# RWKV quarters: products of the joins, the values and the inverse's application laid over four array quadrants, with other work put between them

## The chip, the cores and the metric

The kernel runs on one core of one Trainium2 chip. The metric is the device time of one execution in microseconds (us). The PE (TensorE) makes the matrix products, ACT (ScalarE), DVE (VectorE) and POOL (GpSimd) the rest; SP issues the weight loads. The PE writes into eight PSUM banks of 128 partitions x 512 words. One fp32 product of the program shows as two PE records in the trace, a transpose or a product in the fp32r type as one.

## The reference

The program is three blocks for 512 tokens of width 1024. The change lies in the second block, in an RWKV-7 time mix: 16 heads of width 64, a state per head that is updated token by token.

```python
def step(state, inp):                      # state: heads x 64 x 64
    r_t, w_t, k_t, v_t, a_t, b_t = inp     # a = -kk, b = kk * a_gate
    sa = jnp.einsum('bhvk,bhk->bhv', state, a_t)
    state = (state * w_t[:, :, None, :] + sa[..., None] * b_t[:, :, None, :]
             + v_t[..., None] * k_t[:, :, None, :])
    return state, jnp.einsum('bhvk,bhk->bhv', state, r_t)
...
y = wkv7_scan(r_h, heads(decay), k_h, v_h, -kk, kk * a_h)
y = ((y - mean) * lax.rsqrt(var + GN_EPS)).reshape(B, S, RWKV_DIM)   # a norm per head
y = y * ln_w.astype(f32) + ln_b.astype(f32)
bonus = jnp.sum(r_h * k_h * r_k.astype(f32), axis=-1, keepdims=True) * v_h
y = y + bonus.reshape(B, S, RWKV_DIM)
return (y * g.astype(f32)).astype(z.dtype) # g = sigmoid(gd) @ g2, the gates
```

## The kernel before

The scan is done in chunks of 64 tokens. Within a chunk the tokens' effect on each other is a triangular system of 64 x 64; with its inverse known, the whole chunk is matrix products, and only a short chain of eight state steps runs from chunk to chunk.

The work goes in four quarters (`for q in range(4)` in each engine's program), each for four heads h = 0..3, or 2n + x with n, x in 0, 1. A tile of 128 tokens (c = 0..3) holds two chunks, z = 0 on partitions 0 to 63 and z = 1 on 64 to 127. Most tiles of this stage are `[128, c, h, 64]`: the rows of both chunks on the partitions, and for each tile and head 64 columns. Products of this stage therefore have 64 rows and 64 outputs: each uses one quadrant of the PE array, chosen by the half of the partitions it reads and the half it writes.

After the projections k, r and v of a quarter and the small products low and gram, PE makes the inverse `invt` of each chunk's system. Blocks of 16 come from powers (`pa`, `pd`, up to `pd` of level 3). Two joins then put blocks of 16 together to 32 and of 32 to 64: for each level, `mu` = `e_m` x `invt`, copied by ACT to `mid`; `my` = `inv` x `mid`, added by DVE into `invt`. `inv` is the transpose of `invt`, made by DVE (`turn_inverse`). All of these go in two halves g (tiles 2g and 2g + 1) of eight products of a chunk pair each, made by `pair_of_tiles`. Then:

- `x0` = `ka` x values, copied by ACT into the first 64 columns of `x_a`; `ta` turns `a_r` into the last 64;
- `w` = `invt` x `x_a`, 128 columns, one bank for each tile c, copied out by ACT (c = 0 to 2) and DVE (c = 3) to `w_a`;
- `e` and `s` from `w_a` (DVE adds them up), the gates products (`gates_part`), and `y`;
- `st`, the chain of state steps, between them pieces of the next quarter's k projection (`some_channels`) on PE.

`rwkv_out` turns the result of the quarter before. POOL makes `e_m` (semaphore `between_ready`), multiplies the normed result of the quarter before with its gates (`rwkv_o_ready`) and prepares the gates.

The order of the work is written by hand in every engine's program. Each result of PE is a job with a number; the list of `job` calls gives the order, a job's bank is its number modulo eight, `claim` waits for the reader of the bank's job before, `fill` signals the last product, `wait_full` and `read` stand at the reader, and `wait_read` waits for it. Every matmul of the program goes through line 857 and every transpose of this stage through line 870, every ACT operation through line 1548; so profiles are read by tiles and by time. Of DVE, 2173 is a sum or product of two tensors, 2612 the turning of the inverse, 2658 the copy of w's last bank. Line 694 issues small loads on ACT's queue. The placing of the products is this, before and in the y stage (`both` is the pair of partition halves):

```python
# pair_of_tiles: output half z, from half z
ins = mm(ps(j)[z, at_:at_ + DH], w[z, c, h, :], x[z, c, h, :])
# y: output half z xor x
for n, x, h, _ in heads:
    for z in range(2):
        mm(o[c, n, x][both[z ^ x]], kr[both[z], c, h, :], v_by_head[both[z], c, h, :], c == 0 and n == 0, False)
```

Weights come in pieces: SP loads them, ACT rounds a high part (`weights_hi`), DVE takes the low part (`weights_lo`), each some pieces ahead (`stream_to`).

Of the kernel before, what the change touches and what calls it, by code (L numbers as in the profile page):

```python
# [36 lines left out]
ALU = mybir.AluOpType  # L37
# [65 lines left out]
def build_program(nc, d, x_saved, fc_saved, out):  # L103

    with ExitStack() as ctx:
# [311 lines left out]
        for q in range(4):  # L417
# [23 lines left out]
            for g in range(2):  # L441
                job(q, "pd", g, 3)
            for g in range(2):
                job(q, "x0", g)
            for g in range(2):
                job(q, "mu", g, 0)
            twice(q, "ta")
            for g in range(2):
                job(q, "my", g, 0)
            for g in range(2):  # L450
                job(q, "mu", g, 1)
            for g in range(2):
                job(q, "my", g, 1)
            if q:
                twice(q - 1, "out")
            for c in range(TT):
                job(q, "w", c)
# [3 lines left out]
            job(q, "g", 0)  # L461
            twice(q, "s")
            job(q, "g", 1)
# [390 lines left out]
        def _(pe):  # L854
# [327 lines left out]

            def rwkv_out(q):

                pe.wait_ge(sem("rwkv_o_ready"), q + 1)
                for n in range(2):
                    transposes(J[q, "out", n], [y_q[:, c, n * P:(n + 1) * P] for c in range(TT)])

            def gates_part(q, g):

                j = J[q, "g", g]
                claim(pe, j)
                for c in range(2):
                    tok = slice((2 * g + c) * P, (2 * g + c + 1) * P)
                    mm(ps(j)[:, c * 256:(c + 1) * 256], lo_g1[:, tok], g2_a[:, 256 * q:256 * q + 256], True, False)
                    ins = mm(ps(j)[:, c * 256:(c + 1) * 256], lo_g2[:, tok], g2_b[:, 256 * q:256 * q + 256], False, True)
                fill(j, ins)
# [7 lines left out]
            for q in range(4):  # L1205
# [82 lines left out]
                pe.wait_ge(sem("v_centred"), q + 1)  # L1288
                for g in range(2):
                    for c in (2 * g, 2 * g + 1):  # L1290
                        for x in range(2):
                            wait_read(pe, J[q, "gram", c, x])
                    pair_of_tiles(J[q, "x0", g], g, ka, v_by_head)


                for g in range(2):
                    wait_read(pe, J[q, "pd", g, 3])
                    pe.wait_ge(sem("between_ready"), 4 * q + g + 1)
                    pair_of_tiles(J[q, "mu", g, 0], g, e_m[0], invt)
                for n in range(2):  # L1300
                    transposes(J[q, "ta", n], [a_r[:, n, c, 0, :] for c in range(TT)])
                for g in range(2):
                    pe.wait_ge(sem("inv_turned"), 4 * q + g + 1)
                    wait_read(pe, J[q, "mu", g, 0])
                    pair_of_tiles(J[q, "my", g, 0], g, inv, mid)
                for g in range(2):
                    wait_read(pe, J[q, "my", g, 0])
                    pe.wait_ge(sem("between_ready"), 4 * q + g + 3)
                    pair_of_tiles(J[q, "mu", g, 1], g, e_m[1], invt)
                for g in range(2):  # L1310
                    pe.wait_ge(sem("inv_turned"), 4 * q + g + 3)
                    wait_read(pe, J[q, "mu", g, 1])
                    pair_of_tiles(J[q, "my", g, 1], g, inv, mid)
# [3 lines left out]

                for n in range(2):
                    wait_read(pe, J[q, "ta", n])
                for c in range(TT):  # L1320
                    if c % 2 == 0:
                        wait_read(pe, J[q, "my", c // 2, 1])
                        wait_read(pe, J[q, "x0", c // 2])
                    j = J[q, "w", c]
                    claim(pe, j)
# [3 lines left out]
                    fill(j, ins)  # L1329
# [3 lines left out]
                for g in range(2):  # L1333
                    for z in range(2):
                        claim(pe, J[q, "e", g, z])
# [1651 lines left out]
```

## Time and profile before

| what | value |
|---|---|
| three runs | 1526.01, 1526.58 (median), 1530.64 us |
| the profiled execution, its own time | 1530.57 us |
| its span, first to last instruction | 1528.8 us |
| PE busy | 1494.9 us, 98% |
| DVE, ACT, POOL busy | 890.8, 694.6, 119.5 us |
| mean granted clock of PE | 0.992 of full |

A row of a timeline gives start, duration, engine, line, operation, output and input tiles and shape, and how many instructions are merged in it; in brackets the idle time of the engine before it and what ended that. The duration of a PE row runs to the modelled end of its last product and overhangs the start of the next row a little; the time that a burst costs is the distance of the starts. All SBUF tiles of this stage lie in one buffer, shown as `arena`, some in `extra`. `ACTq` is ACT's queue of issues. Times in the timelines are us from the start of the span. The four quarters' stages of small products end near 399, 494, 584 and 676 us.

### The profile page before, as it was taken

To read this page: it belongs to the slowest core of one execution; us is meant where nothing else is said; L and a number is where in the kernel's file an instruction comes from. 1 tells how busy PE (TensorE), PEld (TensorE's weight loads), DVE (VectorE), ACT (ScalarE), POOL (GpSimd) and SP (SyncE) were. 2 spreads that over 40 slices of the span, in tenths; PEclk is the share of its full clock that TensorE was granted. 3 is DMA by queue.
4 is the path that set the end of the run, shared out by engine and by line. 5 is a ranking of instruction groups with operands and counts; after the bars stand their busy time and mean duration, and the time that the engine had idled before them with its cause. 6 is when DMAs were issued, how large, how long until landed. Compare 5 with 4: busy or idle time off the path is not lost.

```text
span 1528.8 us, 31329 instructions
## 1 busy us (share of the span) xinstructions
PE 1494.9 (98%) x13362; PEld 1227.0 (80%) x13362; DVE 890.8 (58%) x1665; ACT 694.6 (45%) x1267; POOL 119.5 (8%) x78
## 2 busy tenths in 40 slices
PE   6999999999999999999999999999999999999998
PEld 5877867778789797888787778888887888888886
DVE  3658465547475574843347996442456777777223
ACT  5563265573352644434337997422244433334132
POOL 0004000002222142231000000000000000000000
PEclk9999999999999999999999999999999999999999
DMA  6232205331020111207221001232441323232331
GB/s 218 84 111 84 83 29 166 129 100 46 10 79 11 56 38 30 57 11 176 83 63 48 2 2 43 84 110 84 163 138 42 110 83 110 83 110 84 96 111 69
DMA packets 110970, 123.68 MB, mean 81 GB/s; under 512 B 22344, under 2 KB 94664, under 8 KB 110448
## 3 DMA queue, kind: packets, MB, share of 16 engines
q1 hardware_dynamic: 107904, 114.26, 23.8%
q10 hardware_dynamic: 2928, 7.41, 1.4%
q8 instruction: 107, 1.75, 0.5%
q14 instruction: 31, 0.25, 0.1%
HBM read 117.45 MB, written 4.21 MB: 80 GB/s over the span
## 4 chain that ended last, share of the span: by engine, by line
PE 87%; ACT 5%; DVE 4%; issue 2%; DMA 1%; SPq 0%; DVEq 0%; ACTq 0%
PE bank L857 83%; PE bank L870 4%; ACT arena L1548 3%; DVE arena L2173 1%; ACT L1548 1%; DMA arena<-in_x 1%; DVE weights_lo L2173 1%; DMA weights<-in_w_in 1%; ACT weights_hi L1548 1%; DVE arena L2539 0%; DVE arena L2176 0%; DVE arena L2347 0%; DVE arena L2263 0%; ACT extra L1548 0%; ACT h_hi L1548 0%
## 5 line engine op out<-in xcount | busy, mean ns | idle before, releaser
L1548 ACT ACTIVATE arena<-bank 128x512 f32<-128x512 f32 (+3 forms) x399 | 215.1, 568 | 492.0 <-PE bank L857 456.2
L857 PE MATMUL bank<-h_hi,weights_hi 128*128 128x512 f32 x1000 | 400.3, 400 | 4.6 <-DVE weights_lo L2173 2.9
L857 PE MATMUL bank<-h_lo,weights_hi 128*128 128x512 f32 x1000 | 391.4, 391 | 0.0
L857 PE MATMUL bank<-h_hi,weights_lo 128*128 128x512 f32 x1000 | 391.3, 391 | 0.0
L2173 DVE TENSOR_TENSOR weights_lo<-weights,weights_hi 128x1024 fp32r<-128x1024 f32 x179 | 220.4, 1234 | 268.2 <-ACT weights_hi L1548 259.1
L857 PE MATMUL bank<-arena 64*64 64x64 f32 (+6 forms) x6978 | 320.5, 249 | 6.0 <-ACT arena L1548 3.5
L857 PEld LDWEIGHTS bank<-arena 64*64 64x64 f32 (+3 forms) x6978 | 256.4, 140 | 65.0 <-issue 54.6
L1548 ACT ACTIVATE weights_hi<-weights 128x1024 fp32r<-128x1024 f32 x179 | 188.5, 1054 | 150.8 <-PE bank L857 149.2
L857 PEld LDWEIGHTS bank<-h_hi,weights_hi 128*128 128x128 f32 x1000 | 189.0, 189 | 52.3 <-issue 6.8
L857 PEld LDWEIGHTS bank<-h_hi,weights_lo 128*128 128x128 f32 x1000 | 188.8, 189 | 40.2
L857 PEld LDWEIGHTS bank<-h_lo,weights_hi 128*128 128x128 f32 x1000 | 189.1, 189 | 36.6
L1548 ACT ACTIVATE arena<-arena,stat 128x128 f32<-128x128 f32 (+4 forms) x172 | 101.3, 597 | 20.0 <-PE bank L857 10.1
L2173 DVE TENSOR_TENSOR arena<-bank,arena 128x512 f32<-128x512 f32 (+3 forms) x120 | 64.2, 568 | 59.1 <-ACT arena L1548 36.3
L870 PE MATMUL bank<-const,arena 128*128 128x128 f32 x552 | 72.3, 277 | 0.6 <-issue 0.6
L857 PE MATMUL bank<-weights_hi,act_hi 128*128 128x512 f32 x176 | 68.5, 389 | 0.0
L857 PE MATMUL bank<-weights_hi,act_lo 128*128 128x512 f32 x176 | 68.5, 389 | 0.0
L857 PE MATMUL bank<-weights_lo,act_hi 128*128 128x512 f32 x176 | 68.5, 389 | 0.0
L2176 DVE SCALAR_TENSOR_TENSOR ff_c<-arena,par,ff_c 128x512 f32<-128x512 f32 x88 | 66.2, 752 | 3.1
L870 PEld LDWEIGHTS bank<-const,arena 128*128 128x128 f32 x552 | 60.1, 141 | 9.6 <-issue 7.5
L2263 DVE CUSTOM_DVE_ANT_0 arena<-bank,arena 128x128 f32<-128x128 f32 (+3 forms) x144 | 61.9, 486 | 9.2 <-PE bank L857 7.0
L2180 DVE TENSOR_SCALAR arena<-arena,stat 128x512 f32<-128x512 f32 (+4 forms) x174 | 60.3, 407 | 1.8
L2181 DVE TENSOR_SCALAR ff_c<-arena,par 128x512 f32<-128x512 f32 x44 | 24.1, 547 | 60.0 <-ACT arena L1548 59.6
(191 smaller groups left out, 1654.9 us busy)
## 6 DMA issues: line engine op xcount, KB each, us to landing
weights<-in_w_in SPq DMA_DIRECT2D x38, 1024.0 KB, 5.4
weights<-in_ffn_up SPq DMA_DIRECT2D x22, 1024.0 KB, 5.1
weights<-in_ffn_down SPq DMA_DIRECT2D x10, 1024.0 KB, 5.1
weights<-in_w_out SPq DMA_DIRECT2D x4, 1024.0 KB, 5.1
arena<-in_w_out SPq DMA_DIRECT2D x4, 1024.0 KB, 9.3
weights<-in_w_in SPq DMA_DIRECT2D x16, 256.0 KB, 4.6
weights<-in_w_branch_rwkv SPq DMA_DIRECT2D x4, 1024.0 KB, 5.1
weights<-in_w_branch_nsa SPq DMA_DIRECT2D x4, 1024.0 KB, 5.1
```

The source lines that it names most:

```text
L857: return pe.matmul(o, w, x, start=first, stop=last)
L870: ins = pe.transpose(ps(j)[:, i * P:(i + 1) * P], t, ident)
L1548: return act.activation(o, i, f, **kw)
L2173: return dve.tensor_tensor(o, a, b, op)
L2176: return dve.scalar_tensor_tensor(o, a, s, b, op0, op1)
L2180: return dve.tensor_scalar(o, a, s1, None, op0)
L2181: return dve.tensor_scalar(o, a, s1, s2, op0, op1)
L2263: ins = dve.tensor_tensor_reduce(out=unit(probs, 4 * s + n)[:, 0:w], in0=ps(j)[:, at_:at_ + w], in1=table, scale=1.0, scalar=3.0e38, op0=A ...
```

## The change

The products of the joins, of `x0` and of `w` are laid out like those of y: heads with n = 0 write the half that they read, heads with n = 1 the other one. The two n have a bank each, and the four products (n, z) follow one another. What comes out crossed is put back where it is next read: `turn_inverse` turns the inverse of the heads with n = 1 into the other half (three transposes in place of one), so that `my` comes out straight; ACT's copy of x0 and DVE's copy of `w` for n = 1 cross back (two copies of 64 partitions in place of one of 128). Sums and copies of the joins become two of 256 columns for one of 512.

The order changes too. `x0` moves from ahead of mu0 to between the two halves of my0. The gates are cut into four parts, ahead of each half of my1, behind `w` and behind `e`. The first part of the next k projection moves from behind y to ahead of it. DVE makes the sums of pd3 for both halves before it turns either, and takes the two low pieces of the next k behind its `w` copies. ACT copies the first half of the gates ahead of the results of the quarter before, for which it first waits for `rwkv_o_ready`.

```diff
             for g in range(2):
-                job(q, "x0", g)
+                joins("mu", 0, g)
+            twice(q, "ta")
+            joins("my", 0, 0)
+            twice(q, "x0")
+            joins("my", 0, 1)
             for g in range(2):
-                job(q, "mu", g, 0)
...
+                joins("mu", 1, g)
+            job(q, "g", 0)
...
+                joins("my", 1, g)
             if q:
                 twice(q - 1, "out")
...
+            for g in range(2):
+                for n in range(2):
+                    job(q, "w", g, n)
+            job(q, "g", 1)
...
+            def join(q, kind, lev, g, w, x):
+
+                for n in range(2):
+                    claim(pe, J[q, kind, g, n, lev])
+                for c in range(2):
+                    for y in range(2):
+                        for n in range(2):
+                            j, h, at_ = J[q, kind, g, n, lev], 2 * n + y, (2 * c + y) * DH
+                            for z in range(2):
+                                ins = mm(ps(j)[both[z ^ n], at_:at_ + DH], w[both[z], 2 * g + c, h, :], x[both[z], 2 * g + c, h, :])
+                            if c == y == 1:
+                                fill(j, ins)
...
-            def gates_part(q, g):
-
+            def gates_of(q, i):
+
+                g, c = i // 2, i % 2
                 j = J[q, "g", g]
...
+                if c == 0:
+                    claim(pe, j)
+                tok = slice(i * P, (i + 1) * P)
...
-                pe.wait_ge(sem("v_centred"), q + 1)
-                for g in range(2):
...
-                    pair_of_tiles(J[q, "x0", g], g, ka, v_by_head)
...
-                    pair_of_tiles(J[q, "mu", g, 0], g, e_m[0], invt)
+                    join(q, "mu", 0, g, e_m[0], invt)
                 for n in range(2):
                     transposes(J[q, "ta", n], [a_r[:, n, c, 0, :] for c in range(TT)])
+                pe.wait_ge(sem("inv_turned"), 4 * q + 1)
+                joined(q, "mu", 0, 0)
+                join(q, "my", 0, 0, inv, mid)
+                pe.wait_ge(sem("v_centred"), q + 1)
...
+                            for z in range(2):
+                                ins = mm(ps(j)[both[z ^ n], at_:at_ + DH], ka[both[z], c, h, :], v_by_head[both[z], c, h, :])
...
+                pe.wait_ge(sem("inv_turned"), 4 * q + 2)
+                joined(q, "mu", 0, 1)
+                join(q, "my", 0, 1, inv, mid)
                 for g in range(2):
...
+                    joined(q, "my", 0, g)
+                    pe.wait_ge(sem("between_ready"), 4 * q + g + 3)
+                    join(q, "mu", 1, g, e_m[1], invt)
                 for g in range(2):
...
+                    gates_of(q, g)
                     pe.wait_ge(sem("inv_turned"), 4 * q + g + 3)
...
+                    joined(q, "mu", 1, g)
+                    join(q, "my", 1, g, inv, mid)
                 if q:
                     rwkv_out(q - 1)
...
-                    for h in range(4):
-                        for z in both:
-                            ins = mm(ps(j)[z, h * P:(h + 1) * P], invt[z, c, h, :], x_a[z, c, h, :])
...
+                    for c in (2 * g, 2 * g + 1):
+                        for x in range(2):
+                            for n in range(2):
+                                j, h, at_ = J[q, "w", g, n], 2 * n + x, (2 * (c % 2) + x) * P
+                                for z in range(2):
+                                    ins = mm(ps(j)[both[z ^ n], at_:at_ + P], invt[both[z], c, h, :], x_a[both[z], c, h, :])
...
+                gates_of(q, 2)
...
-                gates_part(q, 0)
+                gates_of(q, 3)
...
-                gates_part(q, 1)
...
                 claim(pe, j_next)
+                some_channels(j_next, w_next, (0,))
                 o = {}
...
                 claim(pe, st)
-                some_channels(j_next, w_next, (0,))
...
+            def keep_mid(q, lev, g):
+
+                for n in range(2):
+                    j = J[q, "mu", g, n, lev]
+                    wait_full(act, j)
+                    o = mid[:, 2 * g:2 * g + 2, 2 * n:2 * n + 2].rearrange("p c x v -> p c (x v)")
+                    read(j, run(o, ps(j)[:, 0:256].rearrange("p (c x) -> p c x", c=2), ACT.Copy))
...
+                for n in range(2):
+                    to_heads(J[q, "x0", n], x_a[:, :, 2 * n:2 * n + 2, 0:DH], n)
                 phase_loads(act, "ln", L_LN[q])
                 for g in range(2):
-                    to_pair(J[q, "mu", g, 1], g, mid)
+                    keep_mid(q, 1, g)
+                if q:
+                    act.wait_ge(sem("rwkv_o_ready"), q)
+                copy_out(J[q, "g", 0], g_q[:, 0:2, :].rearrange("p c x -> p (c x)"))
...
+                    dve.transpose(pairs(inv, slice(0, P), 0), pairs(invt, slice(0, P), 0))
+                    for z in range(2):
+                        ins = dve.transpose(pairs(inv, sides[1 - z], 2), pairs(invt, sides[z], 2))
+                    ins.then_inc(sem("inv_turned"), 1)
...
                     sum_into(J[q, "pd", g, 3], g, invt)
-                    turn_inverse(J[q, "pd", g, 3], g)
                 for g in range(2):
                     wait_read(dve, J[q, "pd", g, 3])
...
+                    turn_inverse(g)
...
+                    join_sum(1, g)
+                for g in range(2):
+                    j = J[q, "w", g, 1]
+                    wait_full(dve, j)
+                    for z in range(2):
+                        to, at_ = slice(DH * z, DH * z + DH), slice(DH - DH * z, P - DH * z)
+                        ins = dve.tensor_copy(w_a[to, 2 * g:2 * g + 2, 2:4].rearrange("p c x v -> p c (x v)"),
+                                              ps(j)[at_, :].rearrange("p (c x) -> p c x", c=2))
+                    read(j, ins)
                 stream_to(next_k)
```

## Rows read from the trace of the kernel before

**Rows 1.** The page, parts 1 and 4: PE's share, and the ending chain by engine.

```profile
PE 1494.9 (98%) x13362; PEld 1227.0 (80%) x13362; DVE 890.8 (58%) x1665; ACT 694.6 (45%) x1267; POOL 119.5 (8%) x78
...
PE 87%; ACT 5%; DVE 4%; issue 2%; DMA 1%; SPq 0%; DVEq 0%; ACTq 0%
```

**Rows 2.** Timeline of PE, quarter 3: x0, mu0, then my0 to my1, out, w.

```profile
649.75 2.03 PE L857 MATMUL bank<-extra,arena 64*64 64x64 f32 x64
651.62 2.03 PE L857 MATMUL bank<-arena 64*64 64x64 f32 x64
...
654.60 6.20 PE L857 MATMUL bank<-arena 64*64 64x64 f32 x192
660.74 1.09 PE L870 MATMUL bank<-const,extra 128*128 128x128 f32 x8
661.76 7.77 PE L857 MATMUL bank<-arena 64*64 64x128 f32 x208
```

**Rows 3.** Timeline of PE, quarter 3: gates, y, k projection, first state step.

```profile
671.22 1.99 PE L857 MATMUL bank<-arena 128*128 128x256 f32 x8
673.14 1.16 PE L857 MATMUL bank<-extra,arena 64*64 64x64 f32 x64
674.12 1.11 PE L857 MATMUL bank<-arena 64*64 64x64 f32 x64
675.16 0.50 PE L857 MATMUL bank<-h_hi,weights_hi 128*128 128x512 f32 x1
...
676.06 0.45 PE L857 MATMUL bank<-arena 64*64 64x64 f32 x8
```

**Rows 4.** Timeline of all engines, quarter 3: DVE, ACT and POOL at the joins.

```profile
649.10 0.69 DVE L2173 TENSOR_TENSOR arena<-arena,bank 128x512 f32<-128x512 f32 x1 [0.54 <-PE bank L857]
...
649.83 0.71 DVE L2612 STREAM_TRANSPOSE arena<-arena 128x512 f32<-128x512 f32 x1
...
651.83 0.60 ACT L1548 ACTIVATE arena<-bank 128x512 f32<-128x512 f32 x1 [0.34 <-PE bank L857]
...
653.28 2.36 POOL L2111 TENSOR_TENSOR extra<-extra,arena 128x1024 f32<-128x1024 f32 x1
...
654.72 0.34 ACTq L694 DMA_DIRECT2D arena<-in_g_ln_w  x1
...
655.09 0.45 ACTq L694 DMA_DIRECT2D arena<-in_g_ln_b  x1
655.87 0.69 DVE L2173 TENSOR_TENSOR arena<-arena,bank 128x512 f32<-128x512 f32 x1 [4.01 <-PE bank L857]
```

**Rows 5.** Timeline of all engines, quarter 3: low pieces, w copies, sums of e.

```profile
661.52 2.35 DVE L2173 TENSOR_TENSOR weights_lo<-weights,weights_hi 128x1024 fp32r<-128x1024 f32 x2
...
662.90 0.60 ACT L1548 ACTIVATE arena<-bank 128x512 f32<-128x512 f32 x1 [0.38 <-PE bank L857]
...
665.52 0.69 DVE L2658 COPY arena<-bank 128x512 f32<-128x512 f32 x1 [1.65 <-PE bank L857]
666.45 2.74 DVE L2173 TENSOR_TENSOR arena<-bank,arena 128x256 f32<-128x256 f32 x8 [0.24 <-PE bank L857]
```

**Rows 6.** Timeline of PE, quarter 3: a gram set alone, and gram mixed with pairs.

```profile
630.87 0.90 PE L857 MATMUL bank<-arena 64*64 64x64 f32 x32
631.70 0.50 PE L857 MATMUL bank<-h_hi,weights_hi 128*128 128x512 f32 x1
...
633.29 4.11 PE L857 MATMUL bank<-arena 64*64 64x64 f32 x160
```

**Rows 7.** Groups by shape, whole span: a DVE sum of half the width.

```profile
L2173 DVE TENSOR_TENSOR arena<-bank,arena 128x256 f32<-128x256 f32 x32 | 11.0, 416 | 0.9 <-PE bank L857 0.9
```

**Rows 8.** Timeline of ACT, 684 to 700: copies of 64 partitions, 256 columns.

```profile
690.54 1.53 ACT L1548 ACTIVATE arena<-bank 64x256 f32<-64x256 f32 x4
```

**Rows 9.** Window of PE, quarter 1: length, busy, granted clock, DMA share, GB/s.

```profile
466.00:468.00 2.00, 2.00 (x46) 0.51 0.00 0
```

**Rows 10.** Timeline of PE, quarter 1: x0 at that time.

```profile
467.76 2.80 PE L857 MATMUL bank<-extra,arena 64*64 64x64 f32 x64
```

More of the change, by code:

```diff
@@ L1335, in _ @@
                         claim(pe, J[q, "e", g, z])
+                    for n in range(2):
+                        wait_read(pe, J[q, "w", g, n])
                     for c in (2 * g, 2 * g + 1):
-                        wait_read(pe, J[q, "w", c])
                         for m in range(2):
@@ L1808, in _, with to_heads @@
             run(lo_g2, lo_g2, ACT.Sigmoid).then_inc(sem("lora_ready"), 1)
-            def to_heads(j, o, n=DH):
+            def to_heads(j, o, n):
                 wait_full(act, j)
-                read(j, run(o, ps(j)[:, 0:512].rearrange("p (h x) -> p h x", x=n), ACT.Copy))
+                src = ps(j).rearrange("p (c x v) -> p c x v", c=TT, x=2)
+                for z in range(2) if n else (None,):
+                    to, at_ = (slice(0, P),) * 2 if z is None else (slice(DH * z, DH * z + DH), slice(DH - DH * z, P - DH * z))
+                    ins = run(o[to], src[at_], ACT.Copy)
+                read(j, ins)
+            def keep_mid(q, lev, g):
+                for n in range(2):
+                    j = J[q, "mu", g, n, lev]
+                    wait_full(act, j)
+                    o = mid[:, 2 * g:2 * g + 2, 2 * n:2 * n + 2].rearrange("p c x v -> p c (x v)")
+                    read(j, run(o, ps(j)[:, 0:256].rearrange("p (c x) -> p c x", c=2), ACT.Copy))
             def to_pair(j, g, o):
@@ L1892, in _ @@
                 for g in range(2):
-                    to_heads(J[q, "x0", g], x_a[:, 2 * g:2 * g + 2, :, 0:DH].rearrange("p c h v -> p (c h) v"))
-                for g in range(2):
-                    to_pair(J[q, "mu", g, 0], g, mid)
+                    keep_mid(q, 0, g)
                 for n in range(2):
@@ L2607, in turn_power, with turn_inverse, pairs, join_sum @@
                     dve.transpose(flat(pwt, g), ps(j)).then_inc(sem("powers_turned"), 1)
-                def turn_inverse(j, g):
-                    wait_read(dve, j)
-                    dve.transpose(flat(inv, g), flat(invt, g)).then_inc(sem("inv_turned"), 1)
+                def turn_inverse(g):
+                    two, sides = slice(2 * g, 2 * g + 2), (slice(0, DH), slice(DH, P))
+                    def pairs(t, part, h):
+                        return t[part, two, h:h + 2, :].rearrange("p c h x -> p c (h x)")
+                    dve.transpose(pairs(inv, slice(0, P), 0), pairs(invt, slice(0, P), 0))
+                    for z in range(2):
+                        ins = dve.transpose(pairs(inv, sides[1 - z], 2), pairs(invt, sides[z], 2))
+                    ins.then_inc(sem("inv_turned"), 1)
+                def join_sum(lev, g):
+                    for n in range(2):
+                        j = J[q, "my", g, n, lev]
+                        wait_full(dve, j)
+                        o = invt[:, 2 * g:2 * g + 2, 2 * n:2 * n + 2].rearrange("p c x v -> p c (x v)")
+                        read(j, tt(o, o, ps(j)[:, 0:256].rearrange("p (c x) -> p c x", c=2), ALU.add))
                 turn_low(0)
```

83 lines of the change are left out of this document (38 added, 45 removed).

## The prediction

> **What bounds the kernel now.** I read the page first. The PE is busy 98% of the span and holds 87% of the chain that ended last [rows 1], so time leaves the kernel only where PE time leaves it or where PE is made to wait. Next I read PE's timeline through quarter 3, which stands for the other three, and there the pace of a record (one fp32 product of the program shows as two). Products that `pair_of_tiles` lays on two quadrants, (low half, low half) and (high, high), take 649.75 to 651.62 for 64 records: 1.87 us, 29 ns each [rows 2]. The first half of the y stage, 64 records of the same shape laid on all four quadrants, takes 673.14 to 674.12: 0.98 us, 15.3 ns each [rows 3]. The order in y is the order that the change writes: z inside head, two neighbours into one bank, then two into another, output half z xor x. So the new pace can be read from the old trace.
>
> Last I read DVE and ACT over the same stretch. The reader of a bank starts some 0.2 us (ACT: 651.83 behind the burst that ended at 651.62) or 0.34 us behind the last product of its bank (DVE: 655.87, behind the 0.93 us of my0's first half), and the product that needs its result follows 0.1 us after it. PE shows almost no idle, because each link (product, copy, sum, transpose, product) of one half g hides behind the other half's 0.93 us [rows 2, 4]. With 0.49 us in its place, some links will show.
>
> **The change part by part**, for one quarter, on the clock of quarter 3.
>
> *Removed from PE.* Five sets of 64 records go to 0.98 us each: x0 (1.87), mu0 (651.62 to 654.60 less the 1.02 of eight transposes, 1.96), and my0, mu1 and my1 (654.60 to 660.74, 6.14, of which some 0.5 was links that showed already) [rows 2]. The w products (128 columns) fill a bank every 0.87 us, as the copies behind them show (662.90 to 665.52, first and last of four), 3.5 us from 661.76 [rows 2, 5]. Their new pace is not in the trace alone. The nearest row is gram, which mixes 16 records of 64 and 16 of 128 columns on four quadrants: the burst from 633.29, 4.11 us with the 0.07 by which a burst's shown end overhangs, holds three such sets and two pairs of 0.93, so one set is 0.72 us; less 16 x 15.3 ns, a record of 128 columns is 30 ns, and w is 64 x 30 = 1.9 us [rows 6]. Old: 1.87 + 1.96 + 6.14 + 3.5 = 13.5. New: 5 x 0.98 + 1.9 = 6.8. Saved: 6.7 us a quarter.
>
> *Added to PE.* The gates product is cut from two bursts into four. Whole it takes 671.22 to 673.14, 1.92 us [rows 3]; a gram set standing alone takes 0.83 us (630.87 to 631.70) against 0.72 inside a burst [rows 6], so a detached burst costs 0.1. Four gates bursts of 1.05 for 3.84, and 0.1 each for starts of other bursts that now stand apart: 0.5 in all. `some_channels(0)` takes 0.9 us on either side of y [rows 3]; in its old place it covered the wait for `y_started`. In the new one the eight records of the first state step do (busy 0.45 us [rows 3]), so I put nothing for it; without that cover it would be one drain of PE, at most those 0.45 us.
>
> *Added to DVE and ACT.* A join's sum becomes two of 128x256, 0.42 us each [rows 7] and 0.34 apart in a row (eight in 2.74 [rows 5]): 0.76 instead of 0.69. A turn becomes three transposes. The trace has only 128x512, 0.71 us [rows 4]; sums go from 0.69 to 0.42 with half the width, so I take 0.42, three in a row 1.1 us; the other end is 0.7 each, 2.0 us. A mid copy becomes two of 256 columns; ACT's nearest is 64x256 out of a bank, four in 1.53 us [rows 8], so 0.75 a pair against 0.60. x0 becomes three copies, taken at 0.6 each. The crossing w copies are two of 64x512 on DVE; the nearest is its 128x512 copy, 0.69 us [rows 5], so 1.3 a pair. DVE gets some 4 us more work in a stage in which it was idle for 4.0 us at once [rows 4].
>
> *What of it is on the path.* PE's timetable, from the end of pd3 at 649.75:
> - mu0 g0 waits for the sum of g0, which ends 649.79 [rows 4]: 649.9. mu0 g1 waits for the sum of g1 (bank filled 649.7, sum 650.03 to 650.72): 650.8 to 651.3. PE stands 0.15 and 0.4 us; x0 lay there before. The ta transposes run to 652.4.
> - my0 g0 652.4, its inverse turned at 651.75; x0 652.9 to 653.9; my0 g1 to 654.4; mu1 g0 to 654.85, its sum ready at 654.0.
> - mu1 g1 needs the sum of my0 g1: 654.36 + 0.33 + 0.76 + 0.1 = 655.55. PE stands 0.7 us, then runs to 656.05.
> - gates to 657.1. my1 g0 needs mid g0 of level 1. ACT has by then the ta copies (to 653.7), x0 (to 655.85), the two DMA issues of the ln rows (0.34 and 0.45 us of its queue [rows 4]) and the mid copies: 657.4. PE stands 0.3. Behind the DMA issues wait both mid copies of level 1, and PE for them.
> - my1 g0 to 657.95, gates to 659.0, my1 g1 to 659.5, the out transposes to 660.55: the last sum of g1 ends 660.6, under them and w g0.
> - w to 662.45, gates to 663.5. DVE has brought back w's second bank of g0 by 663.15, that of g1 by 664.4: e 663.5 to 665.5 meets them with 0.3 and 0.1 us to spare. Gates 666.55, s 668.45, `some_channels(0)` 669.35, y 671.4.
>
> The waits sum to 1.55: 6.7 - 0.5 - 1.55 = 4.65, and the first state step starts at 671.4 instead of 676.06 [rows 3]. DVE comes close: with its two low pieces (2.35) moved behind the w copies it ends them at 666.75, the eight sums of e (2.74) at 669.5 [rows 5], the two of s (0.69 each) at 670.8. From there the order is the old one, so nothing is given back later. POOL's rwkv output, which ACT now waits for ahead of the first gates copy, ends at 655.64 [rows 4], before ACT is there. A bank is claimed when the reader eight uses before is done; the closest is w's second bank behind the first gates copy, filled 659.0, read 659.8, needed 660.55. SP draws a weight piece when PE has ended an earlier one, as now.
>
> Quarter 0 has no out transposes; the last sum of g1 then shows for 0.25 us. I put all four at 4.65: 18.6 us. The profiled execution took 1530.57 around a span of 1528.8 and is close to the slowest shown; it would become 1512. It holds one fall of the clock (below). The median, 1526.58, is what a new run is compared with: 1526.6 - 18.6 = 1508.
>
> **The rule against it.** In y the two products that follow each other into one bank lie on different row halves, and the pace is 15.3 ns [rows 3]. The Trainium skill, TensorEngine Tiling (Array Packing), Restrictions and Gotchas, says that different row tiles cannot access the same PSUM bank at once. By that rule each z pair of the joins would go one after the other, and the joins would keep 29 ns or more. The trace speaks against it here.
>
> **The rivals.**
> *Links bind* (0.15). Half-size transposes, sums and copies cost nearly what whole ones do: turn 2.0, join sum 1.3 us. Then DVE is the path from the sum of pd3 on: turns to 654.7, sums 657.3, turns 661.3, my1 g1 661.9, sums 663.9, w copies 666.5, e to 667.6, y to 673.5. Gain 2.6 a quarter, 10 in all: 1516. For: no row of a half-size transpose. Against: sums do shrink with width [rows 7].
> *Links hide better* (0.10). No wait shows and the bursts join without loss: 6.7 x 4 = 26.8: 1500. For: the old order hid nearly all. Against: 0.49 us is shorter than 0.33 + 0.76.
> *It doesn't do what it says* (0.03). The joins stay at 29 ns a record; what is left are the splits, 0.5 a quarter: about 1529, within what can't be told from no change.
> *The clock* (0.07), the other side. In quarter 1 the granted clock falls to the 1.2 GHz level at 466, while PE is shown busy, amid products on two quadrants [rows 9]; a set of 64 records is busy for 2.80 us there instead of 2.03 [rows 2, 10], 0.8 us lost in that set alone. The new order has PE standing in short gaps amid small products. From pd3 to y it holds some 20 us of PE work a quarter; each us of it at the lower level costs one more, so from 4.65 us a quarter on, the gain is gone. If half of it ran so, the kernel would be 10 - 4.65 = 5.4 us a quarter slower: 1548. The Trainium skill, TensorE: Matmul & The Clock Gate, Part 1, has the low clock as the default that activity releases; that would favour a fall in the new gaps. Against it: PE's records of the same stretch in quarter 3 keep their full pace [rows 2, 3], and four-quadrant products and gates leave less of the array idle than what they replace.
>
> **How the numbers follow.** Forecast 0.65, rivals as given. The forecast alone spans 1503 to 1513 (link times by a quarter up or down, one fall of the clock more or less). The low end, 1499, takes in the case without waits; the high end, 1518, the case where the links bind. Beyond lie the clock and the case without effect, 0.1, and some of the unforeseen. A measurement of this kernel tells 0.3%, 4.6 us, from no change. Faster by more: 0.92; within: 0.03; slower: 0.05 (most of the clock's case).
>
> **What would show it.** Right: 64 records of a join in about 1 us; w's banks of a half filled within 0.95 us; the first state step some 21.6 us after pd3 instead of 26.3; a PE gap of 0.7 us ahead of the second mu1 and about 0.3 ahead of my1. Wrong: joins at 29 ns; transposes of 256 columns near 0.7 us; DVE late for e, or for the first state step; a granted clock of half in the joins; the next quarter's projections waiting for low pieces that they did not wait for before.

## The result, and the profile after

| kernel | median, us | executions | against the kernel before, 95% interval |
|---|---|---|---|
| before | 1527.49 | 4 | |
| changed | 1518.83 (1518.43 to 1519.72) | 4 | 0.9944 [0.993, 0.9959] |
| changed, unchanged on another chip (after_again) | 1522.64 (before there: 1528.11) | 10 | 0.9954 [0.9937, 0.9971] |

Faster, by 8.7 us where 18.6 were forecast: 1518.8 lies just outside the range. (One of the ten executions of after_again, at a granted clock of 0.845, is left out of its ratio.) The profiled execution took 1519.72 around a span of 1517.9. The page of the changed kernel, part 1, PE's line, and part 4, the chain by engine:

```profile
PE 1476.1 (97%) x13362; PEld 1203.7 (79%) x13362; DVE 911.2 (60%) x1725; ACT 695.3 (46%) x1283; POOL 119.0 (8%) x78
...
PE 85%; ACT 5%; DVE 5%; issue 2%; DMA 1%; SPq 1%; POOLq 0%; POOL 0%; DVEq 0%; ACTq 0%
```

PE is still the bound; "issue", time in which an engine waits for nothing that the profile shows, has 2% of the chain, as before. PE's busy time fell by 18.8 us and the span by only 10.9 (from 1528.8): PE now stands for some 8 us that it did not stand before. Timeline of PE in quarter 3 of the changed kernel (start, duration, what, idle time before and its releaser):

```profile
637.06 2.70 PE L861 MATMUL bank<-arena 64*64 64x64 f32 x96
640.00 0.69 PE L861 MATMUL bank<-arena 64*64 64x64 f32 x32 [0.24 <-DVE arena L2223]
...
642.16 0.86 PE L861 MATMUL bank<-extra,arena 64*64 64x64 f32 x43
643.21 0.59 PE L861 MATMUL bank<-extra,arena 64*64 64x64 f32 x21 [0.18 <-issue]
643.62 1.19 PE L861 MATMUL bank<-arena 64*64 64x64 f32 x64
645.20 4.51 PE L861 MATMUL bank<-arena 64*64 64x64 f32 x104 [0.39 <-DVE arena L2223]
649.64 1.09 PE L874 MATMUL bank<-const,extra 128*128 128x128 f32 x8
650.67 6.65 PE L861 MATMUL bank<-arena 64*64 64x128 f32 x208
...
658.42 0.58 PE L861 MATMUL bank<-arena 64*64 64x64 f32 x7
658.80 0.28 PE L861 MATMUL bank<-extra,arena 64*64 64x64 f32 x3
...
661.21 0.74 PE L861 MATMUL bank<-arena 64*64 64x64 f32 x34
663.00 0.85 PE L861 MATMUL bank<-arena 64*64 64x64 f32 x38 [1.04 <-issue]
```

pd3 is the first 64 records of the burst at 637.06 and ends at 638.95 at [rows 2]'s 29 ns. The first state step follows the last 30 records of y, at 663.00 + 30 x 0.0153 = 663.46 (the other eight of the 38 are the state step's): 24.5 us after pd3, against 26.3 before and 21.65 forecast. Bursts of the joins do run at about 15 ns: 32 records from 641.65 to 642.16 are 16 ns each, where [rows 2] has 29. But there are stands (stretches in which PE runs nothing) that the forecast does not have, and most have "issue" as releaser: amid x0 (643.21), amid s (the seven records at 658.42 end in a gap up to 658.80), amid y's second half (663.00, behind its record 34). DVE in the same stretch:

```profile
639.86 0.44 DVE L2666 STREAM_TRANSPOSE arena<-arena 128x256 f32<-128x256 f32 x1
640.31 0.89 DVE L2668 STREAM_TRANSPOSE arena<-arena 64x256 f32<-64x256 f32 x2
...
648.10 0.75 DVE L2223 TENSOR_TENSOR arena<-arena,bank 128x256 f32<-128x256 f32 x2 [0.36 <-PE bank L861]
...
651.86 2.81 DVE L2729 COPY arena<-bank 64x512 f32<-64x512 f32 x4 [1.27 <-PE bank L861]
```

A turn is 0.44 + 0.89 = 1.33 (1.1 forecast), a join's sum 0.75 (0.76), four copies of w 2.81 (2.6): near the estimates, where [rows 4] has whole transposes of 0.71. All that PE waits for without a visible reason, whole span, before and changed, and in the changed kernel for DVE's sums (engine, line, releaser: us in total, times, longest):

```profile
PE bank L857 <- issue: 2.2, 3, 1.0
```

```profile
PE bank L861 <- issue: 8.5, 12, 1.4
...
PE bank L861 <- DVE arena L2223: 1.9, 6, 0.4
```

**Where these stands come from.** Part 3 of both pages has this queue of instructions (packets, MB, share):

```profile
q8 instruction: 107, 1.75, 0.5%
```

That is 16 KB a packet. Part 1 counts 13362 products and as many weight loads of PE, 26724 instructions, which over 107 packets is 250 each. In windows of 0.25 us one such packet stands alone as a slice of 66 GB/s (66 x 0.25 is 16 KB). The changed kernel, quarter 3 (window, length, busy time of the engines, PE's granted clock, DMA share, GB/s):

```profile
648.50:648.75 0.25, 0.25 (x3) 0.18 (x1) 0.25 (x2) 0.00 (x0) 0.00 (x0) 1.00 0.34 66
652.50:652.75 0.25, 0.25 (x9) 0.18 (x2) 0.24 (x2) 0.07 (x1) 0.00 (x0) 1.00 0.34 66
656.25:656.50 0.25, 0.25 (x3) 0.22 (x2) 0.25 (x1) 0.00 (x0) 0.00 (x0) 1.00 0.29 66
660.00:660.25 0.25, 0.25 (x5) 0.02 (x3) 0.25 (x2) 0.00 (x0) 0.25 (x1) 1.00 0.35 66
```

One packet about every 4 us, and PE goes on 2.5 to 3 us behind it (656.25, 658.80; 660.00, 663.00). From the end of x0's stand to the end of y's there are 626 records in 19.79 us (PE's window: length, busy and records, clock, DMA share, GB/s):

```profile
643.21:663.00 19.79, 18.13 (x626) 1.00 0.07 17
```

A record is two instructions, a weight load and a product, so 125 records and the waits among them fill one block: five blocks, 3.96 us each on average. Counted on from 643.21, 123 records lead to a stop of 0.35 us inside my1 (647.34, within the row of 645.20), 499 to the one at 658.80 and 626 to the one at 663.00; the bounds between, inside w (652.14) and e (655.52), show no stand. This gave the theory to test: **PE gets its instructions in 16 KB blocks, one per 4 us, and the new order uses them faster.** The rivals: links of DVE and ACT that the records do not name, and the clock.

### The profile page after: what moved, and what is told of

The parts are those of the page before. It is cut to its first block, busy times and chain, and to the rows that moved or that the text cites. A ratio compares the mean times of both kernels' runs of the same rounds, so it can differ in the third digit from the quotient of the medians.

```text
span 1517.9 us, 31464 instructions
## 1 busy us (share of the span) xinstructions
PE 1476.1 (97%) x13362; PEld 1203.7 (79%) x13362; DVE 911.2 (60%) x1725; ACT 695.3 (46%) x1283; POOL 119.0 (8%) x78
## 4 chain that ended last, share of the span: by engine, by line
PE 85%; ACT 5%; DVE 5%; issue 2%; DMA 1%; SPq 1%; POOLq 0%; POOL 0%; DVEq 0%; ACTq 0%
PE bank L861 81%; PE bank L874 4%; ACT arena L1584 3%; DVE arena L2223 1%; ACT L1584 1%; DVE weights_lo L2223 1%; ACT weights_hi L1584 1%; DMA weights<-in_w_in 1%; SPq L806 1%; DVE arena L2589 0%; DVE arena L2226 0%; DVE arena L2397 0%; DMA arena<-in_c_v_mask 0%; ACT extra L1584 0%; DVE arena L2313 0%
## 5 line engine op out<-in xcount | busy, mean ns | idle before, releaser
L1584 ACT ACTIVATE arena<-bank 128x512 f32<-128x512 f32 (+5 forms) x415 | 215.8, 553 | 475.0 <-PE bank L861 437.5
L861 PE MATMUL bank<-arena 64*64 64x64 f32 (+6 forms) x6978 | 304.2, 250 | 14.1 <-issue 7.5
L861 PEld LDWEIGHTS bank<-arena 64*64 64x64 f32 (+3 forms) x6978 | 236.6, 140 | 78.5 <-issue 65.7
```

Of the source, the lines that this page charges most:

```text
L861: return pe.matmul(o, w, x, start=first, stop=last)
L1584: return act.activation(o, i, f, **kw)
```

## The experiments

The stage in this table runs from the second head product of a quarter (the product of 128x2 ahead of pd3) to its third state step, summed over the four quarters, less what the clock took in it (one minus the granted clock, summed over windows of 1 us). It is read from one profiled execution each; the changed kernel's own two profiles differ by 1.0 (121.0 and 120.0), so differences of about 1 us are not read. The ratios are against the kernel before on the same chip.

| run | median, us | ratio, interval | stage, us |
|---|---|---|---|
| before | | | 129.7 |
| changed | 1518.83 | 0.9944 [0.993, 0.9959] | 121.0 |
| after_again | 1522.64 | 0.9954 [0.9937, 0.9971] | 120.0 |
| e1_y_split | 1523.64 | 0.9978 [0.9966, 0.9991] | 122.7 |
| e2_after_half_y | 1515.71 | 0.9933 [0.9912, 0.9954] | 116.8 |
| e3_before_half_y | 1522.89 | 0.9972 [0.9958, 0.9986] | 125.6 |
| e4_pad | 1529.78 | 1.0012 [0.9996, 1.0028] | 124.1 |
| e5_two_quadrants | 1539.24 | 1.0067 [1.0043, 1.0091] | 137.7 |
| e6_old_places | 1526.0 | 0.9987 [0.997, 1.0004] | 125.3 |
| e7_more_between | 1538.94 | 1.0067 [1.005, 1.0084] | |
| e8_short_turn | 1522.54 | 0.9964 [0.995, 0.9977] | 120.9 |
| e9_long_run | 1558.2 (one) | | |
| e10_pad_block | 1532.4 | 1.0032 [1.0017, 1.0047] | 120.7 |
| e12_more_between_again | 1540.7 (one) | | 131.2 |

**e9: the supply by itself.** Ahead of the quarter loop:

```
+            for n in range(2):
+                claim(pe, J[0, "decay", n])
+            for x_of in (lambda n: n // 2 % 2, lambda n: 0):
+                for n in range(320):
+                    x, z, at_ = x_of(n), n % 2, DH * (n // 4 % 8)
+                    mm(ps(J[0, "decay", x])[both[z ^ x], at_:at_ + DH], ident[both[z], 0:DH], ident[both[z], 0:DH])
```

> Ahead of the quarter loop PE gets 320 more products of 64 columns on all four quadrants (640 records, two buffers of 512 columns, the order of y), and behind them 320 of the same on two quadrants; their results are overwritten. Nothing waits for anything in them, so only the array and the supply of instructions are left. Supply theory: on four quadrants the 640 records do not keep 15.3 ns (9.8 us); they stand some 0.3 to 1.2 us about every 125 records, 5 times, together 11.5 to 15 us, with one 16 KB packet of the instruction queue per stand; on two quadrants they run at 29 ns without a stand, 18.6 us. Rival (the stands belong to the joins, their links and banks, not to the instructions): 9.8 us and 18.6 us, neither with a stand.

PE's timeline over it; the burst at 334.35 holds the change from four quadrants to two:

```profile
318.23 3.15 PE L861 MATMUL bank<-const 64*64 64x64 f32 x200 [0.73 <-issue]
322.34 2.10 PE L861 MATMUL bank<-const 64*64 64x64 f32 x128 [0.96 <-issue]
326.34 2.09 PE L861 MATMUL bank<-const 64*64 64x64 f32 x128 [1.91 <-issue]
330.34 2.10 PE L861 MATMUL bank<-const 64*64 64x64 f32 x128 [1.91 <-issue]
334.35 3.13 PE L861 MATMUL bank<-const 64*64 64x64 f32 x128 [1.91 <-issue]
338.07 16.78 PE L861 MATMUL bank<-const 64*64 64x64 f32 x568 [0.60 <-issue]
```

PE waits for no other engine here, and gets exactly 128 records, 256 instructions, per 4.00 us: 2.1 of work and 1.91 of standing, 31 ns a record whatever the array could do. On two quadrants 568 records take 16.78, 29.5 ns each, without a stand: the supply just keeps up with the old layout. In windows of 0.5 us the packets are the slices of 33 GB/s:

```profile
323.50:324.00 0.50, 0.50 (x48) 0.50 (x44) 0.00 (x0) 0.00 (x0) 0.00 (x0) 1.00 0.12 33
...
326.00:326.50 0.50, 0.16 (x9) 0.16 (x12) 0.00 (x0) 0.00 (x0) 0.00 (x0) 1.00 0.00 0
...
327.50:328.00 0.50, 0.50 (x49) 0.50 (x44) 0.00 (x0) 0.00 (x0) 0.00 (x0) 1.00 0.12 33
...
331.50:332.00 0.50, 0.50 (x49) 0.50 (x44) 0.00 (x0) 0.00 (x0) 0.00 (x0) 1.00 0.12 33
```

The engine goes on at 326.34, the next packet comes at 327.5 to 328, its instructions run from 330.34. The stands are longer than the 0.3 to 1.2 that I expected; here no other work lies between. The rival, that such stands come only with the joins' links and banks, has fallen.

**e4 and e10: move the block bounds.** Products of 8 columns ahead of the quarter loop, 32 (64 records, half a block) and 64 (a whole one); the pad itself brings a lower granted clock with it (0.77 over 320 to 335 us in e4), so the places are to be read here, not the times:

```
+            claim(pe, J[0, "decay", 0])
+            for n in range(64):
+                mm(ps(J[0, "decay", 0])[both[0], 8 * (n % 32):8 * (n % 32) + 8], ident[both[0], 0:DH], ident[both[0], 0:8])
```

> The changed kernel with 32 small products (64 records, half a block of instructions) put once ahead of the first quarter, 1 to 3.5 us of PE work by themselves. Supply: every later block ends 64 records earlier in the program, so PE's stands move by 64 records in all quarters: the one in quarter 3 behind record 34 of y's second half goes to about record 34 of y's first half, the one in x0 behind record 43 to mu0 or ta. The time moves by the products' own cost and by up to 3 us either way. Links: the stands stay where they are, time plus 1 to 3.5 us.

> 64 products of 8 columns (128 records) are put ahead of the quarter loop of the changed kernel, twice as many as in the run with the pad of 32: about one 16 KB block of PE's instructions. Supply theory: the blocks' bounds come back to the places that they have without a pad, within a few records (in quarter 3 the stand in the second half of y again, behind about record 30, and none in the first half), and so do the lengths: the stage of the four quarters again near 123 us (124 with the pad of 32); the kernel is some 2 us slower than the changed one for the pad itself. Rival (the stands belong to places in the program): positions do not move in any run, or move anywhere.

The stands in quarter 0's s and y, quarter 2's joins and y, and quarter 3's y, as what follows a stand; without a pad (after_again), then a whole block, then half a block:

```profile
395.71 0.34 PE L861 MATMUL bank<-extra,arena 64*64 64x64 f32 x6 [0.22 <-issue]
399.36 0.71 PE L861 MATMUL bank<-arena 64*64 64x64 f32 x18 [0.51 <-issue]
...
559.60 4.06 PE L861 MATMUL bank<-arena 64*64 64x64 f32 x101 [1.11 <-issue]
575.44 0.21 PE L861 MATMUL bank<-extra,arena 64*64 64x64 f32 x1 [0.29 <-issue]
664.12 0.85 PE L861 MATMUL bank<-arena 64*64 64x64 f32 x38 [0.48 <-issue]
```

```profile
407.68 0.34 PE L861 MATMUL bank<-extra,arena 64*64 64x64 f32 x6 [0.77 <-issue]
411.32 0.71 PE L861 MATMUL bank<-arena 64*64 64x64 f32 x18 [0.52 <-issue]
...
571.97 5.61 PE L861 MATMUL bank<-arena 64*64 64x64 f32 x101 [1.11 <-issue]
589.51 0.21 PE L861 MATMUL bank<-extra,arena 64*64 64x64 f32 x1 [0.29 <-issue]
...
678.41 0.85 PE L861 MATMUL bank<-arena 64*64 64x64 f32 x38 [0.50 <-issue]
```

```profile
673.98 0.63 PE L861 MATMUL bank<-extra,arena 64*64 64x64 f32 x28 [0.67 <-issue]
```

With a whole block each of these stands is back at the same record (x6, x18, x101, x1, x38); with half of one quarter 3's has moved from 30 records before the end of y's second half to 28 before the end of its first: 62 records, for a pad of 64. In quarter 0, counted from the start of the stage, the stands behind records 738 and 865 lie behind 674 and 801 with half a block. The stage is 124.1 with half a block and 120.7 with a whole one, where 123 was expected. A stand belongs to a place in the stream of instructions, not to a step of the computation.

**e8: shorter links.** One of the two crossing transposes of each turn is left out, so a quarter of the inverse's turned tiles stays old:

```
-                    for z in range(2):
+                    for z in range(1):
                         ins = dve.transpose(pairs(inv, sides[1 - z], 2), pairs(invt, sides[z], 2))
```

> The changed kernel with one of the three transposes of every turn of the inverse left out (so half of the inverse of two heads is stale; four turns a quarter, 0.45 us each on DVE). Links: the turns lie on PE's path at both levels, 0.45 to 0.9 us a quarter, 1515.5 to 1517. Supply: PE stands for its instructions anyway, at most the shown wait ahead of the second mu1 (0.4 us) shrinks: 1518 to 1519.

PE's wait ahead of the second mu1 in quarter 3, by its timeline:

```profile
651.71 4.24 PE L861 MATMUL bank<-arena 64*64 64x64 f32 x104 [0.39 <-DVE arena L2223]
```

It is 0.39, as in the changed kernel, and the stage 120.9 against 121.0, with 0.44 us less on DVE in every turn. The median, 1522.5, lies above both expectations, so the stage is what decides here. The turns are not what the gain was lost to; the links through sums and copies were not shortened in any run, but PE's waits that name DVE's sums are the 1.9 us above.

**e5: the layout undone in the new order.**

```
-   ins = mm(ps(j)[both[z ^ n], at_:at_ + DH], w[both[z], 2 * g + c, h, :], x[both[z], 2 * g + c, h, :])
+   ins = mm(ps(j)[both[z], at_:at_ + DH], w[both[z], 2 * g + c, h, :], x[both[z], 2 * g + c, h, :])
```

and the same in x0 and w, with the crossing copies and transposes straight.

> The changed kernel's order, splits and sizes of copies with the old layout: both groups of heads write the half that they read, so the products of the joins, x0 and w go on two quadrants. Supply: the joins go back to 29 ns a record, a block lasts 3.7 us, the stands in the joins go: the time is that of before plus the splits (0.5 us a quarter), 1529. Links: the links hide behind the slower products as they did before, 1529 too. Either way it tells what the layout alone is worth: if the order gave the gain, it would stay near 1519.

PE's timeline in quarter 3:

```profile
653.34 4.09 PE L861 MATMUL bank<-arena 64*64 64x64 f32 x128
...
683.06 0.85 PE L861 MATMUL bank<-arena 64*64 64x64 f32 x38 [0.77 <-issue]
```

The joins have no stand on two quadrants, while y, on four, has its stand at x38 still. The layout is worth 17 us of stage (137.7 to 121.0); the order and the splits without it cost 8 (129.7 to 137.7), of which 3.2 are visible issue idle (3.67 against 0.48). In quarter 3, by the distance of starts, the stage is 1.92 longer than before, and these make it up: the gates in four bursts of 1.06 for two of 1.92 (0.4), the two bursts of my1 alone at 1.08 for 0.93 (0.3), and the stands in s and y (0.29 and 0.97). The time, 1539, is 10 above the 1529 that both theories gave: neither had counted on stands that the order alone brings.

**e6: the gates whole in their old places, the projection piece behind y again.**

```
-                    gates_of(q, g)          (behind each mu1)
-                gates_of(q, 2)              (behind w)
-                gates_of(q, 3)              (behind e)
+                gates_of(q, 0); gates_of(q, 1)      (behind e)
+                gates_of(q, 2); gates_of(q, 3)      (behind s)
```

> The new layout with the gates whole between e and s and between s and y, and the first k piece behind y, as before. Supply: blocks are eaten in one run through the joins, w and e, so more stands there and fewer at s and y: 1521 (1518 to 1525). Links: the links ahead of my1 lose the gates that covered them, 0.4 to 1 us a quarter, the splits' 0.4 come back: 1520. It tells what the gates' and the k piece's new places are worth.

PE's waits over the whole span:

```profile
PE bank L861 <- issue: 6.3, 9, 1.1
PE bank L861 <- DVE arena L2667: 3.9, 7, 0.7
PE bank L861 <- DVE arena L2728: 3.8, 7, 0.8
```

Without the gates between them the joins wait for the turns (L2667), and e for the w copies (L2728), 7.7 us in all, and the stage is 4.3 longer. These places are worth some 4 us; the median, 1526.0 (just outside the 1518 to 1525 expected), fits that.

**e2 and e3: half of y left out** (its products of br with w_a), in the changed kernel and in that before:

```
-                for c in range(TT):
-                    for n, x, h, _ in heads:
-                        for z in range(2):
-                            ins = mm(o[c, n, x][both[z ^ x]], br[both[z], c, h, :], w_a[both[z], c, h, 0:DH], False, False)
```

> The changed kernel without the second half of y (the 64 records a quarter of br x the first half of w_a, so y lacks the part of a chunk's own tokens that goes through w). Links: 64 records at 15.3 ns go, 0.98 us a quarter, 3.9 in all: 1515. Supply: half a block of instructions goes, so the stretch shrinks by half of 4 us, 1.6 to 2.1 us a quarter, 6.5 to 8.5 in all: 1511.

> The same 64 records a quarter left out of the kernel before, whose y shows no stand. Both theories: 0.98 to 1.04 us a quarter, 4 us in all, 1523.5. If it saves as much as in the changed kernel, the supply theory falls.

The stage falls by 4.2 in the changed kernel (3.2 against after_again) and by 4.1 in the kernel before; 64 records of 15.3 ns in four quarters are 3.9. The supply theory had wanted 6.5 to 8.5 from the changed kernel, and on record it was to fall if both kernels saved as much, as they did: taken as written, the two runs speak for the rival. What follows is a reading made after them. The records left out also move the bounds of all later blocks, so other stands change: by quarter 3, 3 x 64 records, one and a half blocks, are gone, and its stands lie behind records 288 (1.05 us, at the joins) and 789 of the stage, as they do in e4 with half a block more, where the changed kernel has them behind 227, 350, 726 and 853. So a saving in one place need not show in the sum. These runs did not tell the two apart; e9 and e10 did.

**e1, e7 and e12: work of few instructions between the halves of y.** e1 puts one piece of the next quarter's k projection there:

```
                         mm(o[c, n, x][both[z ^ x]], kr[both[z], c, h, :], v_by_head[both[z], c, h, :], ...
+                some_channels(j_next, w_next, (1,))
...
-                        some_channels(j_next, w_next, (m,))
+                        ins = some_channels(j_next, w_next, (m + 1,))
```

e7 adds three pieces of the next quarter's first projection ahead of, between and behind the halves. e12 is the same kernel once more, for a profile.

> Two theories of why the change gained 8.7 us and not 18.6. Supply: PE stands because its instructions come too slowly; they come in blocks of 16 KB (256 instructions, some 125 PE records), and a stretch of four-quadrant products eats a block in about 2 us, while the next is usable some 4 us behind the start of the one before. Links: DVE and ACT links are longer than estimated and PE waits for them. Here the last of the eight full-size pieces of the next k projection moves from the end of the state chain to between the two halves of y; PE's work is the same and no link of the joins changes. Supply: the stand within y (1.0 us in quarter 3, 0.8 in quarter 0) shrinks by up to the piece's 0.7 us in each quarter, 1516 us (1515 to 1517.5). Links: nothing changes, 1518.8 within 0.7.

> The changed kernel with more full-size work drawn into the runs of small products: the last piece of the next k projection between the halves of y, and three pieces of the one after it (in the first three quarters) ahead of y, between its halves and behind it, taken out of the projections that follow. PE's work is the same. Supply: they fill the stands of y and the first state step, 1 to 2 us a quarter, 1513.5 (1511 to 1516). Links: nothing to gain in y, 1518.8; changes of tile size between the pieces cost 0.1 each, 1520.

> The kernel with three pieces of the next quarter's first projection around y once more, for a profile, since its times (1536 to 1541 us) are some 14 us above those of the kernel with the split alone. Supply theory: the stands in y are gone (the pieces hold few instructions), and what is lost shows as another wait of PE: the buffer of the next quarter's first projection is held open through the state steps, so the buffer eight uses later is claimed late, and PE waits for ACT or DVE at the head of the next quarter, some 3 to 5 us in each of quarters 1 to 3. Rival (more pieces among the bursts bring the clock down): no new wait, the granted clock at the 1.2 GHz level for 6 us or more inside y and the state steps.

In e1 the stand in y's second half is gone in quarters 0 and 3. The stage holds 0.9 us more work a quarter, 3.6 in all, and is 1.7 longer than that of the changed kernel (2.7 against after_again), so 0.9 to 1.9 is won in it; PE's waits for ACT over the span grow by 1.4 (5.1 against 3.7), which may be the piece that is missing at the state steps. The median, 1523.6, lies above both expectations, and the clock has a part in that: the executions of e1 ran at a mean granted clock of 0.987 to 0.993, and in the profiled one (1524.6 us at 0.988) it took some 18 us, in that of the changed kernel (1517.9 at 0.993) some 11. e7 too missed both expectations, by 19 to 25 us. In e12 the stand is gone from quarter 0's y too, and PE waits at the head of the next quarter:

```profile
PE bank L863 <- ACT arena L1599: 15.7, 9, 4.0
```

12 us more than the 3.7 of the changed kernel, 4 in each of three quarters: the buffer of the next quarter's projection is held open through the state steps, and the use eight later comes late, as expected. Around each of these waits the granted clock falls to the 1.2 GHz level as well. The first and the second (PE's timeline, then windows with length, busy time, granted clock, DMA share and GB/s):

```profile
420.27 0.76 PE L863 MATMUL bank<-h_hi,weights_hi 128*128 128x512 f32 x1 [3.99 <-ACT arena L1599]
```

```profile
422.00:424.00 2.00, 2.00 (x7) 0.58 0.00 0
...
518.00:520.00 2.00, 2.00 (x7) 0.50 0.00 0
520.00:522.00 2.00, 2.00 (x6) 0.50 0.00 0
```

So the recorded rival, the clock, has a share in the time of e12, though not inside y; the executions of e7 ran at 0.986 to 0.989. Filling the stands gave nothing back here. No version that does all the work beats the changed kernel.

**after_again: the clock.**

> The changed kernel itself, unchanged, on the chip of the two runs beside it, for a distribution of its time and granted clock. If its four executions so far (1518.4 to 1519.7 at a mean clock of 0.993 to 0.994) are typical: median 1519, ratio 0.9944. If the clock falls more often in the new order (its relatives run at 0.987 to 0.993, the kernel before at 0.990 to 0.996): median 1521 to 1524, mean clock near 0.990, and some 2 to 4 us of the missing gain are the clock's.

Executions at a mean granted clock of 0.993 or 0.994 took 1518.2 to 1520.2 (3), those of the kernel before 1525.3 to 1529.9 (9); at 0.989 to 0.991 1522.6 to 1524.5 (5) against 1528.1 to 1532.7 (7, from 0.990). At a like clock the gain is 7 to 8 us either way. The changed kernel was at 0.991 or below in five of nine, that before in seven of 21, so the medians there differ by only 5.5; whether the new order brings the clock down more often so few executions do not settle. In the first comparison the changed kernel ran at 0.993 to 0.994, so there the missing gain is not the clock's.

## Why the prediction was wrong

**The pace** was right: the joins run at about 15 ns a record on four quadrants with row-half pairs into one bank, and the rival of no effect and the rule about banks that would have kept them at 29 ns have fallen.

**The step that failed** is PE's timetable, "The waits sum to 1.55: 6.7 - 0.5 - 1.55 = 4.65": each burst was costed at the array's pace and only waits for other engines were added. A term is missing, the supply of PE's instructions. From the end of x0's stand to the end of y's the timetable has 17.4 us (653.56, x0's record 43 from 652.9 on, to 670.94, 30 records ahead of the 671.4); it took 19.79, five blocks. These 2.4 us, and 0.45 up to the end of the first of these stands (4.26 from pd3's end instead of 3.81), are the 2.85 that quarter 3 lost (24.5 less 21.65). By the distance of starts, the stands in x0, my1, s and y are 0.39, 0.33, 0.28 and 1.25 of it, 2.25 together. The other 0.6 is no supply: bursts of 32 records that stand alone take some 0.62 for the 0.5 of the timetable, and e stops 0.24 amid its two halves, behind DVE's last w copy (it ends at 654.67); less what the waits for links came short. Over the four quarters the stands without releaser are some 9 us by the distance of starts, under 1 before, and the gain missing in the stage is 9.8. The gain per quarter is 26.3 - 24.5 = 1.8 there, and 8.8 of stage over all four (129.74 to 120.98), as much as the whole measured gain.

The trace of before could have warned of it: a record is two instructions, so [rows 3]'s 15.3 ns was a pace for 64 to 128 records between longer work, not one for 600 in a row. I read it from one burst and used it for a stretch.

**The waits for links** came near the forecast. The brackets leave out what the row before overhangs; by the distance of starts PE stood 0.45 for the 0.4 ahead of the second mu0 and 0.59 for the 0.7 ahead of the second mu1, although the turns were longer (1.33 for 1.1). The 0.3 ahead of my1 did not come: its first two records follow the gates at once, and the stop behind them is a block's bound. The prices of w (1.91 for 1.9) and of a gates burst (1.06 for 1.05) were right too.

**The rivals.** *Links bind* has the nearest time, 1516, by a mechanism that did not come: it wanted turns of 2.0 and sums of 1.3, which took 1.33 and 0.75, and e8's shorter turns gained nothing. That its time is near is luck. *Links hide better* fell with the sum. *The clock* at the joins did not come: their windows in quarter 3 show 1.00, and before and after have one fall in the stage each, in quarter 1, that took 1.7 us. None of the rivals was the supply; the range's high end, 1518, came from the links and stood 0.8 short.

## What to carry to other kernels

When an edit makes a burst of small products faster, count its instructions as well as its columns: here PE was given 256 per 4.0 us, so records of a weight load and a product passed at 29 to 31 ns each in the long run, and what the array gains beyond that comes back as stands with no releaser. A short burst in an old trace shows the array's pace, not the supply's; look in the profile for the instruction queue's packets and for idle time put down to "issue". A long product with few instructions among the short ones can let the next block come in time (e1's stands in y were gone), but it may be the cover of another wait where it came from.

## What the runs showed of the hardware

A block of 16 KB was usable 2.4 to 3.0 us behind its packet (e9 and quarter 3 of the changed kernel), and from one stand's end to the next it took 4.00 us (e9). On two quadrants 128 records took 3.8 us without a stand; why the blocks come a little faster there is not settled. Pairs of products on different row halves that write one bank ran at 15 to 16 ns a record (the burst at 641.65), and DVE's transposes of half the size took 0.44 us for 0.71. The Trainium skill, Runtime: NRT & Kernel Launch, Instruction fetch mechanics, has instructions fetched in blocks of 16 KiB, 256 instructions, while the engine runs the block before, with the cost of crossing a boundary mostly hidden. The size agrees with the 128 records between stands in e9; hidden it was at 29.5 ns a record and not at 15.3, where each crossing cost 1.91 us.
